# Hybrid attention and expert layer: reordered input projections, query turning and indexer products beside the query products, causal mask added to the attention logits

## What is computed

```
mod = silu(c) @ w_ada + b_ada                       # 6 x 1024, one row for all tokens
h = rmsnorm(x) * (1 + scale1) + shift1
q_a, k_a, v_a, q_b, k_b, v_b, q_i, k_i, w_i, g_a, g_b = split(h @ w_in)
A: a[t,s] = sig(z_ts) * prod_{s<j<t} (1 - sig(z_tj)), s < t      # stick breaking, 8 heads
B: score = sum_h w_i[h] * relu(q_i[h] . k_i); keep the top 128 keys of each query
   softmax over the kept keys of (q_b . k_b / 8 + relative bias) # 8 heads, one shared key head
x = x + gate1 * ((sig(g_a) * (oA @ w_o_a) + sig(g_b) * (oB @ w_o_b)) @ w_out)
x = x + gate2 * moe(rmsnorm(x) * (1 + scale2) + shift2)          # 16 experts, 2 per token
```

## Time and profile before

| | |
|---|---|
| median of 3 runs | 805.81 us (804.68 to 807.87) |
| profiled execution, its own time | 804.75 us |
| its span | 802.8 us |
| granted TensorE clock, mean | 0.988 of full speed |
| busy: TensorE | 747.3 us (93%) |
| busy: VectorE | 615.5 us (77%) |
| busy: ScalarE | 429.9 us (54%) |
| busy: GpSimd | 109.2 us (14%) |
| DMA | 184.9 MB, 230 GB/s over the span |

### The profile page before, as it was taken

How to read it: one execution, slowest core, us unless ns; L and a number is a source line. 1 busy time by engine, 2 the same in 40 slices (tenths; PEclk the granted TensorE clock), 3 DMA queues, 4 the chain that set the end, 5 groups by cost and what they waited for, 6 DMA issues and landing times.

```text
span 802.8 us, 9975 instructions
## 1 busy us (share of the span) xinstructions
PE 747.3 (93%) x3617; PEld 569.3 (71%) x3619; DVE 615.5 (77%) x805; ACT 429.9 (54%) x516; POOL 109.2 (14%) x91
## 2 busy tenths in 40 slices
PE   3899999999999898999999988999999999999992
PEld 3777687776665555667888864788888887888782
DVE  5876886533999958653567657899999999999991
ACT  5433215357575443556423433776677777676760
POOL 4110000000010000002000011013233132413111
PEclk9999999999999999999999999999999999999997
DMA  9929996110130131105438246999999999999983
GB/s 268 353 79 383 386 362 229 52 53 1 53 106 1 55 103 53 53 7 196 138 116 298 111 176 209 415 399 373 385 387 386 387 387 386 387 385 381 372 289 56
DMA packets 87307, 184.93 MB, mean 230 GB/s; under 512 B 8112, under 2 KB 27672, under 8 KB 85216
## 3 DMA queue, kind: packets, MB, share of 16 engines
q1 hardware_dynamic: 79200, 156.29, 51.9%
q0 software_dynamic: 8064, 28.09, 12.2%
HBM read 171.74 MB, written 12.62 MB: 230 GB/s over the span
## 4 chain that ended last, share of the span: by engine, by line
PE 50%; DVE 28%; issue 7%; DMA 7%; ACT 5%; DVEq 1%; POOL 0%; SPq 0%; ACTq 0%; POOLq 0%
PE ps L666 13%; PE ps L668 12%; PE ps L667 12%; DVE w_lo L1963 8%; DMA raw<-in_w_gate 3%; DVE score L1783 3%; DVE m L1782 2%; DVE ys L2083 2%; ACT w_hi L1506 2%; DMA raw<-in_w_in 2%; DVE w_lo L1602 2%; PE ps L924 1%; DVE accm L1664 1%; DVE score L1769 1%; PE ps L940 1%
## 5 line engine op out<-in xcount | busy, mean ns | idle before, releaser
L1963 DVE TENSOR_TENSOR w_lo<-raw,w_hi 128x2048 fp32r<-128x2048 f32 x80 | 179.7, 2284 | 5.6 <-ACT w_hi L1506 5.6
L1506 ACT ACTIVATE w_hi<-raw 128x2048 fp32r<-128x2048 f32 x80 | 151.2, 1915 | 11.1 <-DMA raw<-in_w_gate 4.8
L666 PE MATMUL ps<-w_lo,hgT_hi 128*128 128x512 f32 x256 | 103.4, 404 | 4.6 <-DVE hgT_lo L2105 1.5
L666 PE MATMUL ps<-act_lo,w_hi 128*128 128x512 f32 x232 | 98.3, 424 | 5.1 <-DVE act_lo L1647 3.9
L667 PE MATMUL ps<-w_hi,hgT_lo 128*128 128x512 f32 x256 | 100.2, 391 | 0.0
L668 PE MATMUL ps<-w_hi,hgT_hi 128*128 128x512 f32 x256 | 100.0, 391 | 0.0
L668 PE MATMUL ps<-act_hi,w_hi 128*128 128x512 f32 x232 | 91.1, 393 | 0.0
L667 PE MATMUL ps<-act_hi,w_lo 128*128 128x512 f32 x232 | 91.0, 392 | 0.0
L1244 ACT ACTIVATE w_hi<-raw 128x2048 fp32r<-128x2048 f32 (+2 forms) x29 | 52.0, 1796 | 71.9 <-DMA raw<-in_w_in 48.8
L1602 DVE TENSOR_TENSOR w_lo<-raw,w_hi 128x2048 fp32r<-128x2048 f32 (+2 forms) x29 | 61.9, 2144 | 33.0 <-ACT w_hi L1244 32.8
L619 POOL DMA_INDIRECT out<-ys,slot_tok x15 | 48.9, 3257 | 159.9 <-DVE ys L2083 159.9
(11 more groups left out here) (283 smaller groups left out, 1361.8 us busy)
## 6 DMA issues: line engine op xcount, KB each, us to landing
raw<-in_w_down SPq DMA_DIRECT2D x32, 1024.0 KB, 15.7
raw<-in_w_gate SPq DMA_DIRECT2D x30, 1024.0 KB, 17.7
raw<-in_w_up SPq DMA_DIRECT2D x18, 1024.0 KB, 16.2
raw<-in_w_in SPq DMA_DIRECT2D x16, 1024.0 KB, 6.4
raw<-in_w_ada SPq DMA_DIRECT2D x16, 1024.0 KB, 7.2
raw_late<-in_w_up SPq DMA_DIRECT2D x14, 1024.0 KB, 18.2
raw<-in_w_ada SPq DMA_DIRECT2D x8, 512.0 KB, 6.7
raw_early<-in_w_ada SPq DMA_DIRECT2D x8, 512.0 KB, 6.5
```

The costliest lines, as they stand in the source:

```text
L666: pe.matmul(o, a[0], b[1], start=start, stop=False)
L1506: act.activation(e_hi[s_][:, :], e_raw[r][:, :], ACT.Copy).then_inc(e_top, 1)
L1963: dve.tensor_tensor(e_lo[s_][:, :], e_raw[r][:, :], e_hi[s_][:, :].bitcast(F32), ALU.subtract).then_inc(e_split, 1)
```

## The change

The projections come in the order qi, ka, qa, va; the chunks of w_ada are spread (0, 0, 2, 3, 5, 6, 0, 0), so that the order of arrival is qi0 qi1, 2 x ada, ka0, 3 x ada, ka1, 5 x ada, qa0, 6 x ada, qa1, va0 va1. A segment waits for each bank by itself. The sums of ada go into quarters of the columns of one bank: four products with 32 columns of ones. The three turnings and the indexer products of query tiles 1 and 2 (eight) are issued between the half banks of qa, followed by the two sums; they use the banks that ka held. VectorE scores these tiles and runs the 16 rounds of tile 1 before stage A; it normalises the rows of branch B in two parts, between chunks. In stage A the mask product moves from `suffix` to `z`, which makes the product with `before` unnecessary; two rounds a step instead of four. Six gate triples move ahead of the first logits (FILL_T), and FILL_B shifts by six.

```
-        SEGS = [("misc", 1, None), ("qb", 0, False), ("qa", 1, True), ("ada1", 0, None),
-                ("ka", 1, True), ("ada2", 1, None), ("qi", 0, True), ("va", 1, False)]
+        SEGS = [("misc", 1, None), ("qb", 0, False), ("qi", 0, True), ("ka", 1, True), ("qa", 0, True), ("va", 1, False)]
...
+        N_TURN = 3
+        EARLY_SIDE = [("tr", n, 0) for n in range(N_TURN)] + [("idx", 1 + n // HP, n % HP) for n in range(2 * HP)]
+        SIDE_AT = 2
+        ADA_AT = SIDE_AT + len(EARLY_SIDE)
+        N_SIDE = HP
...
-        FILL_B = [4 * (len(STEPS) - 1) + 4 * (p + 1) for p in range(len(UNITS))]
+        FILL_T = 4 * (len(STEPS) - 1) + 6
+        FILL_B = [FILL_T + 4 * (p + 1) for p in range(len(UNITS))]
...
+            def ada_sums(part):
+
+                pe.wait_ge(chunk_split, first[f"ada{part}"][-1] + 1)
+                pe.wait_ge(early_sb, len(EARLY_SIDE) - 1)
+                for j in range(4):
+                    last = pe.matmul(ps[5 + part][32 * j:32 * j + 32, :], ones[:, 0:32],
+                                     acc[part % 2][:, 512 * j:512 * j + 512], start=True, stop=True)
+                last.then_inc(ada_ps, 1)
...
+            def early_side(n):
+
+                kind, a, hp = EARLY_SIDE[n]
+                b0 = 4 + 2 * (n % 2)
+                if n == 0:
+                    pe.wait_ge(qk_norm, 1)
+                    pe.wait_ge(evac[1], half_before("va"))
+                elif n >= 2:
+                    pe.wait_ge(early_sb, n - 1)
...
+            def beside_qa(half_group):
+                if SIDE_AT <= half_group < ADA_AT:
+                    early_side(half_group - SIDE_AT)
+                elif ADA_AT <= half_group < ADA_AT + 2:
+                    ada_sums(half_group - ADA_AT + 1)
+
+            seg("qi", H)
+            pe.wait_ge(bias_sb, 2)
+            seg("ka", H)
+            seg("qa", H, None, beside_qa)
```

ScalarE (lines without a sign are unchanged):

```
             high(next(todo))
-            act.wait_ge(st_bias, 16)
+            act.wait_ge(qk_var, 1)
+            act.activation(st[:, :, :], st[:, :, :], ACT.Sqrt, bias=epsc[:, 0:1], scale=1.0 / DH).then_inc(qk_sd, 1)
             high(next(todo))
-            seg_copy("qa", qaT, SCALE)
+            seg_copy("qi", qiT)
             high(next(todo))
-            mod_rows(1)
             high(next(todo))
             seg_copy("ka", kaT)
+            for n in range(5):
+                early_side(n)
             high(next(todo))
-            mod_rows(2)
+            for n in range(5, 8):
+                early_side(n)
             high(next(todo))
```

VectorE:

```
-            raw_chunks(first["va"][0] - N_EARLY - 1)
-
-            dve.wait_ge(evac[0], half_before("ada1"))
+            raw_chunks(first["ka"][0] - N_EARLY)
+
+            dve.wait_ge(evac[0], half_before("qi"))
+            dve.wait_ge(evac[1], half_before("ka"))
...
             dve.tensor_reduce(st[:, :, :], qk_sq[:, :, :, :], AX.X, ALU.add).then_inc(qk_var, 1)
+            raw_chunks(first["ka"][1] - first["ka"][0])
             dve.wait_ge(qk_sd, 1)
...
-            raw_chunks(3)
+            raw_chunks(first["qa"][1] - first["ka"][1])
...
+            early_side(0)
+            early_side(1)
+            raw_chunks(1)
+            for q in range(2, 5):
+                early_side(q)
+            raw_chunks(1)
+            for q in range(5, 8):
+                early_side(q)
+            topk_rounds(TOPK // 8)
+            raw_chunks(1)
             softplus(0)
```

More of the change, by code:

```diff
@@ L579, in _ @@
                                    pattern=[[-1, P]], channel_multiplier=1).then_inc(score_cut, 1)
[L580 to L584, removed]
+            cut_future(1)
+            cut_future(2)
+            for part in range(2):
+                pool.wait_ge(ada_sb, part + 1)
+                pool.dma_start(mod_d[part][0].rearrange("(j n) -> j n", j=4), modrow[part][0:P:32, :]).then_inc(st_mod, 16)
+            pool.wait_ge(st_bias, 16)
+            pool.wait_ge(early_ps, N_TURN)
+            toep_load(0, ld_toepA)
+            cut_future(3)
             pool.wait_ge(s_ps, len(STEPS))
@@ L697, in seg @@
                             last.then_inc(w_used, 1)
[L699 to L707, removed]
+                        if after:
+                            after(8 * ci + 2 * m + 1)
+            def ada_sums(part):
[5 more added lines that the diff above has]
+                last.then_inc(ada_ps, 1)
             pe.wait_ge(early_ok, 1)
@@ L802, in _ @@
                 mq_part(u)
[L803 to L807, removed]
             def head(t, h, c0, c1):
@@ L817, in z @@
                 for r in range(2):
-                    last = pe.matmul(zt[m % 2][:, r, 0:S - P * i], head(kaT, 2 * hp + r, P * i, P * i + P),
-                                     head(qaT, 2 * hp + r, P * i, S), start=True, stop=False, skip_group_check=True)
+                    pe.matmul(zt[m % 2][:, r, 0:S - P * i], head(kaT, 2 * hp + r, P * i, P * i + P),
+                              head(qaT, 2 * hp + r, P * i, S), start=True, stop=False, skip_group_check=True)
+                for r in range(2):
+                    last = pe.matmul(zt[m % 2][:, r, 0:P], identb[:, :], neg_ge[:, :], start=False, stop=False,
+                                     skip_group_check=True)
                 last.then_inc(z_ps, 1)
@@ L857, in av_a, with side_task @@
                 last.then_inc(oa_ps, 1)
[L859 to L877, removed]
+            def side_task(hp):
+                if hp:
+                    pe.wait_ge(side_sb, hp)
+                for r in range(2):
+                    last = pe.matmul(sd[:, r, :], head(qiT, 2 * hp + r, S - P, S), kiT[DH * r:DH * r + DH, :],
+                                     start=True, stop=True, skip_group_check=True)
                 last.then_inc(side_ps, 1)
@@ L1294, in seg_copy, with mod_row, early_side @@
                     act.activation(dst[:, m, :], bank(name, m)[:, :], ACT.Copy, scale=scale).then_inc(evac[half], 1)
[L1296 to L1303, removed]
+            def mod_row(part):
+                act.wait_ge(ada_ps, part)
+                act.activation(modrow[part - 1][:, :], ps[5 + part][:, :], ACT.Copy).then_inc(ada_sb, 1)
+            def early_side(n):
+                kind, a, hp = EARLY_SIDE[n]
+                act.wait_ge(early_ps, n + 1)
+                b0 = 4 + 2 * (n % 2)
+                if kind == "idx":
+                    q = n - N_TURN
+                    if q >= 2:
+                        act.wait_ge(score_ok, 2 * (q - 1))
+                    act.activation(rel_early[q % 2][:, :, 0:P * (a + 1)], psum[:, b0:b0 + 2, 0:P * (a + 1)], ACT.Relu
+                                   ).then_inc(early_sb, 1)
+                elif a < 2:
+                    act.activation(qbT[:, 2 * a:2 * a + 2, :], psum[:, b0:b0 + 2, :], ACT.Copy, scale=SCALE
+                                   ).then_inc(early_sb, 1)
+                else:
+                    act.activation(kbT[:, :], ps[b0][:, :], ACT.Copy).then_inc(early_sb, 1)
             act.wait_ge(seg_ready, seg_done("misc", 0))
@@ L1773, in side_task, with early_side @@
                     rounds.extend((a, r) for r in range(TOPK // 8))
+            def early_side(q):
+                _, a, hp = EARLY_SIDE[N_TURN + q]
+                dve.wait_ge(early_sb, N_TURN + q + 1)
+                score_heads(a, hp, rel_early[q % 2])
+            def side_task(hp):
+                assert all(a != 1 for a, _ in rounds)
+                dve.wait_ge(side_sb, hp + 1)
+                score_heads(3, hp, rel)
             def topk_rounds(count):
@@ L1854, in _ @@
             dve.wait_ge(oa_ps, HP)
+            assert not rounds
             rows(0)
@@ L1861, in _ @@
                 gate_splits(FILL_A[-1] if p == 0 else FILL_B[p - 1])
-                topk_rounds(0 if p < 4 else 2)
                 if p >= 3 and p % 2:
                     ob_low((p - 3) // 2)
-            assert not rounds
             gate_splits(128)
```

144 lines of the change are left out of this document (69 added, 75 removed).

## The result

The changed kernel is slower: 822.82 us (median of 4 runs, 820.02 to 824.26) against 806.72 beside it (4 runs), ratio 1.0199 with a 95% interval of 1.0171 to 1.0228. The forecast was 815.2 with a range of 801 to 822, so the direction was right and the size too small; the time lies 0.8 us above the range. The profiled execution took 820.02 (span 818.2, before 802.8). It was the fastest of the four, so of the 7.6 us by which the median missed, only 5.8 (820.02 against 814.2 in the sum) are in this trace. Executions of one and the same kernel differ too: on the chip of the first experiments 21 of the kernel before took 803.5 to 810.9 us.

A forecast was written before the change was run, and what follows sets the result against it. TensorE was taken to set the time nearly everywhere. Terms -4.8 - 3.1 + 1.6 + 16.4 + 1.7 - 3.9 + 1.5 = +9.4 us on 804.75 gave 814.2, as a median 815.2; range 801 to 822.

The forecast's parts named there:

- Ada sums: Projections, TensorE: two sums of 6.9 us in all become 2.1 with four strips at once, -4.8 us.
- VectorE's queue, loads and ScalarE's order: Projections: qa1 lands at 130.8, ka's copies stand behind its high part, TensorE waits 14.8 us in qa; +16.4 us.
- Clock behind it: Projections, after the 14.8 us wait in qa: TensorE's granted clock stays low, +1.7 us, ends 1.7 and 3.4.
- Stage A, -3.9: Stage A: TensorE's waits of 3.4 and 1.1 us go, a gate copy of 0.6 falls here; -3.9 us.
- Stage B, +1.5: Stage B: -5.5 us for an old wait, its clock and a gate copy, +7.0 for new waits from shifted gates.
- Loads on time: Rival, projections: the queue makes up for VectorE's pause, qa1 lands at 122.8, turning 8.2 us earlier; 807.0 us, chance 0.10.
- Stage B covered: Rival, stage B: ScalarE's order there is covered, so the 7.0 us of new waits don't come; 808.2 us, chance 0.08.
- Strips one after another: Rival, projections: the four products of an ada sum take 3.45 us as before, +4.8; 820.0 us, chance 0.08.
- Dense rows that hide waits: Rival, stages A and B: TensorE's busy rows hide 20 us of waits on VectorE, which relief gives back; 795, chance 0.11.
- a late chunk 13: Projections, loads: chunk 13 takes the median 7.2 us to land instead of 5.0, 2.2 us more.

The follow-up runs named there:

- both repairs together: The changed kernel with the copies of ka and of the first five side tasks ahead of qa1's high part, and FILL_T not shifted: 798.12 us, ratio 0.9872.

## Why the prediction was right and wrong

*Ada sums, -4.8: right.* From the sum to the next triple it is 1.0 us (161.84 to 162.84) where it was 3.45. The four strips run at once, as the Trainium skill has it ("TensorEngine Tiling (Array Packing)", Tiling Modes: four independent tiles of 128 x 32); a row of this trace now shows it.

*VectorE's queue, loads and ScalarE's order, +16.4: right, 0.8 too much.* The wait before qa0 was 1.5 (forecast 1.6), the high of qa1 at 131.24 (near 131), the copies of ka at 133.06 (near 133), the wait 14.1 (14.8). The edits of ScalarE's order and of the normalisation show both links of the chain, the order and the load.

*Clock behind it, +1.7: about right.* The first turning and two triples took 3.83 us (135.24 to 139.07), the second and two triples 2.27 (139.07 to 141.34): 1.6 lost.

*The first stretch as a whole* was 0.95 over the terms; to which of them it belongs isn't known. The forecast's milestone for stage A, 187, was its own slip: 171.3 and 18.9 give 190.2, and 191.1 was measured.

*Stage A, -3.9: 0.7 too much, and the size is in part luck.* The waits went as said. "In z they cost no more than in the suffix" was wrong: the experiment with this part alone has the 3.4 us of waits go and 2.1 come back as work. Something that the sum didn't have made up for most of it. With the gates not shifted, stage A takes 98.64 us; with this part alone on the kernel before it takes 107.45. That is 8.8 less where 7.1 of side tasks left, and both have the same gate triples and the 1.1 on `ab`. The 1.7 more may be the changes of form that left together with the side tasks; no run separates them.

***Stage B, +1.5: this is the step that failed; it was +6.3.*** The mechanism and the places were right: units 4, 8 and 12 and before `oa0`. What was wrong is the price of the six triples' shift. Without the shift, stage B was forecast to win 4.9 us (the wait of 3.2 and the low clock of 1.7), and the run without it shows 4.6 (95.38 to 90.79). The shift itself was forecast at 6.4 (new waits of 7.0 less 0.6 for a gate copy) and cost 10.9. Two sizes were missed in it.

First, the new waits. They were put at "1.3, 1.5 and 1.7" and "about 2.5", 7.0 in all. They were 1.74, 1.96, 2.16 and 2.86, and one more of 0.16 at 379.75, 8.9 in all. At unit 4 the chain was sized right (5.6 us from the gate copy at 312.17 to the end of L1896, forecast from 5.5), but what TensorE had to cover it with was 3.9 us (to 316.07), not 4.2. For the last wait the forecast's own terms, 0.5 + 1.9 + 0.3 + 1.1 - 0.9, add up to 2.9 and not to 2.5; 2.86 was measured.

Second, the clock. The forecast took away the low clock of before behind one wait (1.7) and put none behind four new ones. Behind two of them it was low: 4 us at 0.68 and 4 at 0.90, 4 at 0.65 and 4 at 0.92 are 3.4 us lost. These 3.4, which the forecast had at nothing, and the 1.9 of longer waits are 5.3; less 0.5 in smaller things that is the 4.8. Without the shift neither is there.

*The rivals.* Loads on time: refuted by the trace and by the moved normalisation. Stage B covered: refuted. Strips one after another: refuted. Dense rows that hide waits: not borne out, but tested with less relief than the forecast had. VectorE's busy time in stage A fell from 85.7 us to 69.5, by 16 and not by 32: of the 48 rounds of top-k only 38 ran in stage A before (10 were left for stage B), and 30 wider ones run there now. The window of stage A up to the gates is 97.9 us, close to the 97 of the forecast, far from the 92 that would have spoken for the rival, and both repairs together stayed above its 797 us.

*The range* reached up to 822 for the strips (820.0) and a late chunk 13; neither came true. What lay above the forecast is stage B's 4.8, smaller misses elsewhere in the trace, and that the median lies 2.8 us above the profiled execution, which the trace doesn't show (the forecast had added 1.06).

## What to carry to other kernels

A copy that frees a bank must not stand in an engine's queue behind work that waits for a load: list, for each engine, what is queued behind each wait for a DMA and who needs it; here one line moved behind three others was worth 12.7 us. A small shift in where filler work falls (six triples) can be worth as much, since it decides whether 2.3 us of ScalarE's work (312.17 to 314.46) run ahead of or behind a short critical chain. And a forecast with several short waits of TensorE has to price the clock behind each, not only behind the longest.

## What was not expected of the hardware

Waits of about 2 us were enough for the granted clock to fall, but not always. In the changed kernel it fell to 0.68 behind 1.74 us of idleness and to 0.65 behind 2.16, and stayed at 1.00 behind 1.96 and behind 2.86. With the side tasks' copies moved as well, the same four waits stood 11.9 to 13.4 us earlier, and it stayed up behind the 1.74 and fell behind the 2.16 and the 2.86:

```profile
354.00:358.00 4.00, 4.00 (x14) 1.93 (x12) 2.21 (x7) 0.07 (x1) 0.00 (x0) 0.63 0.54 168
378.00:382.00 4.00, 4.00 (x13) 2.97 (x12) 0.42 (x1) 3.53 (x4) 3.30 (x5) 0.65 0.74 241
```

Four of the traces have these four waits: the changed kernel's, the two with ScalarE's copies moved and the one with the normalisation moved. In them the clock fell behind the 1.74 once, behind the 1.96 never, behind the 2.16 four times and behind the 2.86 twice. So the length of such a wait alone doesn't tell whether it costs about 1.7 us more; when it falls seems to matter. The Trainium skill ("TensorE: Matmul & The Clock Gate", Part 1: The HAM clock gate) says that the window in which the chip watches TensorE runs freely and isn't reset when a kernel starts, which would fit; no run here tests it.
